# A second batch of seven-product column pairs in a hybrid layer's input projection, with the heads in another order

## The reference

```python
def hybrid_layer(x, w_in, norm_gain, lb, hgrn_gain, rel_bias, w_out, cos, sin):
    h = rmsnorm(x, norm_gain)                       # x: (1, 1024, 2048) float32
    proj = jnp.einsum('bsd,de->bse', h, w_in)       # w_in: (2048, 59 * 128)
    aq, af, ai, ag, bq, bk, bv, bg, cq, ck, cv, cg = split_columns(proj)
    ya = hgrn2_group(aq, af, ai, lb, hgrn_gain).astype(x.dtype) * jax.nn.silu(ag)   # 6 heads
    yb = band_attention_group(bq, bk, bv, rel_bias).astype(x.dtype) * jax.nn.silu(bg)  # 5 heads
    yc = retention_group(cq, ck, cv, cos, sin).astype(x.dtype) * jax.nn.silu(cg)    # 5 heads
    y = jnp.concatenate([ya, yb, yc], axis=-1)
    return x + jnp.einsum('bse,ed->bsd', y, w_out)  # then one more rmsnorm
```

## Time and profile before

| what | value |
|---|---|
| median of the runs | 1776.33 us |
| the profiled execution's own time | 1775.74 us |
| its span in the trace | 1773.9 us |
| TensorE busy | 1743.0 us, 98% |
| DVE, POOL, ACT busy | 1107.9, 763.1, 626.4 us |
| DMA | 323.08 MB, mean 182 GB/s |
| mean granted TensorE clock | 0.997 |

### The profile page before, as it was taken

One profiled execution on the slowest core, in us unless ns is written; L12 is line 12 of the kernel. 1 busy time (PEld: TensorE's weight loads), 2 busy tenths in 40 slices (PEclk: granted clock), 3 DMA queues, 4 the chain that ended last, 5 costly groups with the idle time before them and its releaser, 6 DMA issues.

```text
span 1773.9 us, 27559 instructions
## 1 busy us (share of the span) xinstructions
PE 1743.0 (98%) x10704; PEld 1444.8 (81%) x10704; DVE 1107.9 (62%) x1641; ACT 626.4 (35%) x923; POOL 763.1 (43%) x545
## 2 busy tenths in 40 slices
PE   7999999999999999999999999999999999999996
PEld 6888888888888788887887888888888877888885
DVE  6857665554668766565555356555655448778886
ACT  4423344332435132231331233333544233333442
POOL 4544444444455544334344433333334430355452
PEclk9999999999999999999999999999999999999998
DMA  7767777685988523323323332233433369778876
GB/s 252 231 226 255 241 236 256 226 261 179 301 268 271 168 71 126 101 74 109 113 72 102 127 109 85 96 96 112 133 117 102 93 207 344 256 247 264 282 248 230
DMA packets 160710, 323.08 MB, mean 182 GB/s; under 512 B 18362, under 2 KB 19135, under 8 KB 160580
## 3 DMA queue, kind: packets, MB, share of 16 engines
q1 hardware_dynamic: 146314, 276.26, 47.7%
q10 hardware_dynamic: 14266, 45.05, 7.2%
HBM read 275.08 MB, written 46.15 MB: 181 GB/s over the span
## 4 chain that ended last, share of the span: by engine, by line
PE 95%; DVE 2%; ACT 1%; DMA 1%; issue 0%; POOL 0%; SPq 0%; DVEq 0%; ACTq 0%; POOLq 0%
PE prj L821 36%; PE prj L800 32%; PE prj L1092 15%; PE mix L960 2%; PE mix L943 2%; PE mix L840 1%; PE mix L885 1%; PE mix L953 1%; PE mix L913 1%; PE mix L916 1%; PE mix L902 1%; PE mix L1013 1%; PE mix L991 1%; PE mix L1016 0%; PE mix L1002 0%; DVE arena L2245 0%
## 5 line engine op out<-in xcount | busy, mean ns | idle before, releaser
L767 POOL TENSOR_SCALAR w_hi<-w_sum 128x512 fp32r<-128x512 f32 x119 | 189.5, 1592 | 502.5 <-DMA w_sum<-in_w 490.6
L800 PE MATMUL prj<-in_hi,w_hi 128*128 128x512 f32 x840 | 329.7, 392 | 9.5 <-DVE w_lo L1697 8.5
L800 PE MATMUL prj<-in_lo,w_hi 128*128 128x512 f32 x840 | 328.4, 391 | 0.0
L800 PE MATMUL prj<-in_hi,w_lo 128*128 128x512 f32 x840 | 328.3, 391 | 0.0
L821 PE MATMUL prj<-mv_hi,w_hi 128*128 128x512 f32 x928 | 300.7, 405 | 1.8 <-DVE mv_lo L1766 1.8
L753 POOL TENSOR_TENSOR w_sum<-in_raw,in_raw 128x512 f32<-128x512 f32 x150 | 202.4, 1350 | 211.0 <-PE prj L800 201.1
L821 PE MATMUL prj<-mv_lo,w_hi 128*128 128x512 f32 x928 | 287.4, 391 | 0.0
L821 PE MATMUL prj<-mv_hi,w_lo 128*128 128x512 f32 x928 | 286.2, 390 | 0.0
L821 PEld LDWEIGHTS prj<-mv_lo,w_hi 128*128 128x128 f32 x928 | 174.2, 188 | 38.1
L821 PEld LDWEIGHTS prj<-mv_hi,w_lo 128*128 128x128 f32 x928 | 174.2, 188 | 38.0
L800 PEld LDWEIGHTS prj<-in_hi,w_hi 128*128 128x128 f32 x840 | 158.5, 189 | 44.0 <-issue 8.9
(11 more groups left out here) (175 smaller groups left out, 2371.8 us busy)
## 6 DMA issues: line engine op xcount, KB each, us to landing
in_raw<-in_wi SPq DMA_DIRECT2D x360, 256.0 KB, 3.2
raws<-in_wo SPq DMA_DIRECT2D x184, 256.0 KB, 3.9
w_sum<-in_w SPq DMA_DIRECT2D x116, 256.0 KB, 3.0
arena<-z_scratch ACTq DMA_DIRECT2D x56, 512.0 KB, 3.9
y_in<-y_scratch SPq DMA_DIRECT2D x80, 256.0 KB, 4.6
z_scratch<-acc_in SPq DMA_DIRECT2D x60, 256.0 KB, 3.9
z_scratch<-stage SPq DMA_DIRECT2D x26, 512.0 KB, 4.4
x_even<-in_xT SPq DMA_DIRECT2D x44, 256.0 KB, 4.0
```

The costliest lines, as they stand in the source:

```text
L767: nc.gpsimd.tensor_scalar(w_hi[q][:], w_sum[q][:], 1.0, None, ALU.mult).then_inc(w_hi_done, 1)
L800: last = nc.tensor.matmul(out, wt[wslot(n)][:, i % GRAN, :], mv[j % 2][:, i, :], start=(i == 0 and wt is w_hi and mv is in_hi), stop=(i == ...
```

## The change

Fourteen of the 29 plain tiles become seven further pairs with seven products: 49 steps of 24 matmuls, each step two slots of 12 (`mid_product`), so there are 98 + 15 * 8 = 218 slots and the mixers' stages hang between all of them. The seven combinations of x of the first batch are stored to DRAM as they are made (`store_set`, 7 * 8 * 2 blocks of 256 KB) and loaded again into `mv_hi` and `mv_lo` (`load_set`). Weights of the second batch come as in the first, by two or four `in_raw` loads a step; POOL makes sums and low parts, ACT the high parts, placed in ACT's stream by `until(slot)`, which issues them up to three slots ahead. DVE's `until(slot)` places the accumulates and the low rows of x. Accumulated half tiles are stored unscaled (`store_mid_spill`) and scaled when they land. All sixteen rows of x for the plain tiles are loaded and split at the end of this batch (`H_DUE`).

Order of heads: five attention heads (slots 2 to 61), retention heads 0 to 2 (64 to 87), six state-space heads (`A_AT`, the first at 89, the others 17 apart from 108 on), retention heads 3 (201) and 4 (209). Before, retention head 4 began 6 slots behind head 3's second sum of squares.

```diff
 IN_PAIRS = 15
...
-STD = TO - IN_TILES
+MID_PAIRS = 7
+STD0 = IN_TILES + 2 * MID_PAIRS
+MID_STEPS = 7 * MID_PAIRS
+MID_SLOTS = 2 * MID_STEPS
+STD = TO - STD0
...
-A_FROM, A_EACH, B_FROM, B_EACH = -4, 20, 121, 12
-A_LATE = 2
-LEVEL_AT = [8, 9, 11, 12, 13, 15, 16]
-C_AT = [183, 192, 201, 210]
+SLOTS = MID_SLOTS + 2 * NG * STD
+A_AT = [89, 108, 125, 142, 159, 176]
+LEVEL_AT = [8, 9, 10, 11, 12, 14, 15]
+LEVEL_AT_SLOW = [8, 9, 11, 12, 14, 15, 17]
+B_FROM, B_EACH = 2, 12
+C_AT = [64, 72, 80, 201]
+FIRST_ORDER = [1, 2, 0, 3]
...
+H_DUE = [88, 89, 90, 91, 91, 93, 95, 97, 100, 100, 101, 101, 101, 102, 103, 103]
...
+            def store_mid_spill(k):
+                v, p, c = mid_spills[k]
+                sp.wait_ge(in_acc_done, v + 1)
+                sp.dma_start(z_dram[2 * p + c[0]][:, half(c[1])], in_acc(p, c)).then_inc(z_mid[p - IN_PAIRS], 16)
...
+            def store_set(j, i):
+                sp.wait_ge(in_comb_lo, HK * j + (i + 1 if j > 0 else HK))
+                for n, mv in enumerate((in_hi, in_lo)):
+                    sp.dma_start(comb_dram[j, i, n], mv[j % 2][:, i, :].bitcast(F32)).then_inc(comb_out[j % 2], 16)
...
+            def load_set(j, i):
...
+                for n, mv in enumerate((mv_hi, mv_lo)):
+                    sp.dma_start(slot(mv, j, i).bitcast(F32), comb_dram[j, i, n]).then_inc(set_in[j % 2], 16)
...
+            def mid_product(n, rows):
+                st = n // 2
+                j = in_at(st)[0]
+                out = bank(st)
+                pe.wait_ge(w_split, n + 1)
+                pe.wait_ge(set_in[j % 2], 256 * (j // 2 + 1))
+                for i in rows:
+                    for wt, mv in ((w_hi, mv_hi), (w_hi, mv_lo), (w_lo, mv_hi)):
+                        last = nc.tensor.matmul(
+                            out, wt[wslot(n)][:, i % GRAN, :], slot(mv, j, i),
...
-            for slot_at, part in ((223, c_ktr), (224, c_scores), (225, c_vtr), (227, c_state), (229, c_out)):
-                put(slot_at, part(last_c))
-            put(231, c_ss(last_c, 0))
+            for slot_at, part in ((-9, c_ktr), (-8, c_scores), (-7, c_vtr), (-5, c_state), (-3, c_out)):
+                put(SLOTS + slot_at, part(last_c))
+            put(SLOTS - 1, c_ss(last_c, 0))
+            for st in range(IN_STEPS, ALL_STEPS):
+                pe.wait_ge(in_acc_done, st - 3)
+                for q in range(2):
+                    mid_product(2 * st + q, range(GRAN * q, GRAN * q + GRAN))
+                    stages[2 * (st - IN_STEPS) + q]()
...
+            def until(slot):
+                while due["hi"] < min(IN_GRANULES + slot + 4, ALL_GRANULES):
+                    in_w_high(due["hi"])
+                    due["hi"] += 1
+                while due["row"] < KB and H_DUE[due["row"]] <= slot:
+                    h_high(due["row"])
+                    due["row"] += 1
...
+            def until(slot):
+                while due["step"] < ALL_STEPS and 2 * (due["step"] - IN_STEPS) + 2 <= slot:
+                    in_accumulate(due["step"])
+                    due["step"] += 1
+                while due["row"] < KB and H_DUE[due["row"]] <= slot:
+                    h_low(due["row"])
+                    due["row"] += 1
```

More of the change, by code:

```diff
@@ new lines, in _ @@
+            load_x(HK)
+            store_mid_two(ALL_STEPS - 4)
+            load_x(HK + 1)
+            load_std_w(ALL_GRANULES)
+            store_mid_two(ALL_STEPS - 3)
+            load_x(HK + 2)
+            load_std_w(ALL_GRANULES + 1)
+            store_mid_two(ALL_STEPS - 2)
+            load_x(HK + 3)
+            load_std_w(ALL_GRANULES + 2)
+            for k in range(2):
+                load_x(k)
+            load_std_w(ALL_GRANULES + 3)
+            for k in range(2, GRAN):
+                load_x(k)
@@ L653, in _ @@
+            store_mid_two(ALL_STEPS - 1)
+            for k in range(HK + 4, KB):
+                load_x(k)
+            for n in range(ALL_GRANULES + NG, W0):
                 load_std_w(n)
-                g, q = divmod(n - IN_GRANULES, NG)
-                t = IN_TILES + g - 2
-                if IN_TILES <= t < DIRECT and q == (0 if t == DIRECT - 1 else 1):
+                g, q = divmod(n - ALL_GRANULES, NG)
+                t = STD0 + g - 2
+                if STD0 <= t < DIRECT and q == (0 if t == DIRECT - 1 else 1):
@@ new lines, in a_unit @@
+                until(b + 9)
+                if u > 0:
+                    store_y(u - 1, a_pos(u - 1))
+                until(b + 10)
+                until(b + 11)
+                sigmoid_exp(m + 1)
+                sigmoid_ln(m + 1)
+                until(b + 12)
+                sigmoid_inv(m + 1)
+                for slot in range(b + 13, b + kdtr_at - 1):
+                    until(slot)
+                if u < A_HEADS - 1:
+                    act.wait_ge(silu_done, m + 2)
+                    load_z(a_tile(u + 1) + 1, T1, z1_in)
@@ L1513, in c_unit @@
[L1513 to L1516 removed]
+                    if end:
+                        load_z(a_tile(0), B, z0_in)
+                    else:
+                        act.wait_ge(filled[1], c_m1(i) + 2)
+                        act.wait_ge(c_qd, i + 1)
+                        load_z(c_tile(i + 1), CQK, z0_in)
+                        until(b + 2)
+                        partner(i + 1)
@@ new lines, in c_unit @@
+                until(b + 2)
+                act.wait_ge(drained[0], c_m0(i) + 2)
+                if not end:
+                    act.dma_start(dec, dec_d[i + 1]).then_inc(cdec_in, 16)
+                until(b + 3)
+                if late:
+                    sigmoid(m)
+                elif not end:
+                    load_z(c_tile(i + 1) + 1, VT, z2_in)
+                until(b + 4)
+                norm_first(1, c_m1(i) + 3, m + 1, c_norm(i))
+                until(b + 5)
+                if i < EARLY - 1:
+                    scaled_k(i + 1)
+                    act.wait_ge(silu_done, m + 1)
+                    load_z(c_tile(i + 1) + 2, T1, z1_in)
```

808 lines of the change are left out of this document (449 added, 359 removed).

## The result

The changed kernel takes 1808.38 us (1807.07 to 1808.94), the kernel before 1776.68 us on the same chip: a ratio of 1.0178, 95% interval 1.0161 to 1.0196. The forecast was 1801, slower, in a range of 1778 to 1819. The profiled execution took 1808.01 us with a span of 1806.2 us. A further run of the same kernel, made beside the experiments, gave 1804.84 us and 1.0171 (1.0156 to 1.0186).

A forecast was written before the change was run, and what follows sets the result against it. TensorE, busy 98% of the span, was taken as the bound. From 1775.74 us, savings of 38.1 and 3.3 us against added waits, slow clock and DMA summed to +24.7, so 1801 us for the median, range 1778 to 1819.

The forecast's parts named there:

- Term 1: TensorE's matmuls: 168 fewer at 0.2267 us each, -38.1 us.
- Term 2: Old handover to plain tiles: its stall goes, -3.3 us.
- Term 3: New handover at the first state-space head, slots 88 to 105: load and store round trips delay TensorE, +36 us (33 to 42).
- the floor by DVE's work: Handover slots 88 to 105: DVE's 61.6 us of work alone sets a floor of 13.6 us.
- Term 4: First retention head, slot 64: the weight's high part stands on ACT behind `scaled_k`, +5.7 us (4.3 to 7).
- Term 5: Retention heads 0 to 2: one slot less between sum of squares and transposes, twice 1.0, +2.0 us.
- Term 6: Last retention head: 15.15 us from sum of squares to rotation, covered by only twelve matmuls, +12.4 us (11 to 13).
- Term 7: Clock: matmuls run at the lower rate after long stalls, at three or four places, +6 us (0 to 12).
- Term 8: First batch's DMAs: added stores need 385 GB/s in about 24 steps, +3 us (0 to 15).
- Term 9: Other five state-space heads: fourth level's operand barely ready, +1 us (0 to 5); attention heads 0.
- the signs that the prediction gave: TensorE waits rise from 16 to over 60 us; over 5 at slots 94, 95, 12 at last retention head, some 6 at 64.
- the rival by `load_set`: Second batch's products wait for `load_set`, some us at each of seven changes of combination: 1810 us, chance 0.05.

The follow-up runs named there:

- e6: Changed kernel with the q tile's load and x rows 4 to 7 loaded earlier, rows of index 4 on due three slots later; 1790.61 us, ratio 1.0089.
- e7: Changed kernel with one extra, never read DVE pass over each of the sixteen rows of x; 1815.36 us, ratio 1.0225.
- e10: e9 with the first three weight loads of the plain tiles one place earlier on SP; 1771.33 us, ratio 0.9972.
- the control: The changed kernel run again without an edit, on the chip of the single-edit runs; 1804.84 us, ratio 1.0171.
- e8: e6 with x rows reordered further, slot 64's high part ahead of `scaled_k`, and accumulates between attention heads later; 1783.90 us, ratio 1.0046.
- e1: Changed kernel with the last retention head's rotation made early, ahead of head 3's norm; 1797.88 us, ratio 1.0117.
- e9: e8 with the last retention head's rotation early, behind both low parts of the squares; 1771.21 us, ratio 0.9976.
- e2: Changed kernel with the q tile's load ahead of the forget gate's first exponential on ACT, first state-space head; 1802.24 us, ratio 1.0142.

## Why the prediction was right

- **Term 1** (-38.1): slots of twelve keep their 2.72 us in both kinds of tile; no run tested the term alone. **Term 2** (-3.3) was mis-read: the chain left TensorE for that long, but its own wait was 1.8 us, the rest was matmuls still running.
- **Term 3** (+36, 33 to 42): 29.2 us of waits and about 8 us of slow matmuls, 39 us in the stretch. The waits were 4.4 us (forecast 7.7), 6.9 (about 11), 1.9 (3), 8.0 (8) and 7.8 (6). The first two were over-sized: the q tile's load was issued at 11.8 us and not at 14.8, and the low part for slot 95 was done at 33 and not at 37. The mechanism, round trips and not DVE's sum, is shown by e6 and e7; the floor by DVE's work shows in e10, at 20 us and not at 13.6.
- **Term 4** (+5.7): 3.34 us of waiting and 2.3 of slow matmuls, these in the change and not in the control. The wait was over-sized: one accumulate row of 0.68 us stood ahead of the rotation and not a pair, and the rotation's first multiply took 1.22 us in place of the 2.34 of the kernel before. The releaser was as argued (e8).
- **Term 5** (+2.0): twice 0.93 us. **Term 6** (+12.4): 11.26 us, with 2.0 of slow transposes and matmuls behind it. e1 and e9 show that the cover was what lacked.
- **Term 7** (+6, 0 to 12): under-sized, about 13 us in the change (2.3 at slot 64, 8.5 in the handover, 2 at the last head) and 11 in the control (0, 8.4, 3). That idle time brings the low rate, as the skill has it, is what every wait of over 4 us shows here. "Stalls of 3.3 us showed no drop" rested on the same mis-reading as term 2, for that wait was 1.8 us; a wait that did last 3.34 us brought it in the change and not in the control.
- **Term 8** (+3, 0 to 15): 0. The first batch ends within 0.2 us of where it did. Two windows of it in the changed kernel (columns as above) hold 386 and 402 GB/s with TensorE busy throughout; the second had 365 before:

```profile
150.00:165.00 15.00, 15.00 (x68) 12.43 (x67) 10.87 (x18) 7.09 (x12) 7.54 (x6) 1.00 1.04 386
470.00:490.00 20.00, 20.00 (x90) 16.57 (x89) 14.43 (x23) 8.52 (x15) 9.05 (x7) 1.00 1.05 402
```

  Of the two limits in the Trainium skill, "DMA: Bandwidth & Descriptors", Where 436 GB/s comes from, 358 GB/s did not bind here: the 402 GB/s lie between it and the fabric's 435. The prediction could have read this from its own row, since the 365 GB/s of the earlier trace rows are above 358 too.
- **Term 9** (0 for the attention heads, +1): the step that failed. "A `landed` multiply less on each tile" balances the two accumulate rows in the mean, but not at the place: between two attention heads DVE has no slack, and 1.36 us show at three places, with 1.8 us at the first head, whose cause no run tested, and 0.5 us more, 6.6 us in all. The other state-space heads and retention head 3 took 3.9 us where 1 was given.

Of the signs that the prediction gave, the waits rose from 16 to 69 us as it said; those at slots 94 and 64 came at 4.4 us for over 5 and 3.3 for some 6, that at slot 95 at 6.9 and that at the last head at 11.3 us. No wait stands at a change of combination in the second batch, so the rival by `load_set` is out. The sum without term 7 is 1794.4, not 1794.6.

Terms 2, 7 and 9 were too small by some 18 us together, the waits of 3, 4, 6 and 8 too large by 13. That leaves 4 to 5 us; the other 2 to 3 lie in the stretches of the table and in no term. The time came out 7 us above the forecast and inside the range in part by luck, because the misses cancel; the main step, a handover made long by round trips in the streams' order, held.

## What to carry to other kernels

Moving work from TensorE is worth its matmuls only where other engines' streams are laid out for it: here 38 us saved brought 53 us more of waits and 13 of slow matmuls, and seven edits of order alone took 34 to 37 us off. A handover between two phases is costed by walking its round trips (load, scale, activate, split, multiply) in the order in which each stream issues them, since a load that stands behind a wait it does not need makes two chains into one. And removing one wait of several in a row shows little; the last of them to fall shows what the floor is. A stretch that got shorter must be split into waits and slow matmuls before the gain is put down to the edit, as e2 shows.
